# Attention scores of a hybrid decoder: one 32-row matmul per head at four row positions, into four banks, in place of masked copies of the keys

## What is computed

```
att      = einsum('bnthd,bnshd,bntshd->bnhts', q, k, decay)      # causal
o_intra  = einsum('bnhts,bnshv->bnthv', att, v)
o_inter  = einsum('bnthd,bnhdv->bnthv', q * exp(b), S_start)
S        = exp(b_last) * S + sum_s (k * exp(b_last - b)) v
o        = o * rsqrt(mean(o^2) + eps)                            # per head
```

## Time and profile before

| | |
|---|---|
| median of 3 runs | 1743.29 us (1737.36 to 1917.84) |
| the profiled execution | 1752.2 us |
| its span on the slowest core (core 0) | 1750.7 us |
| spans of the other cores | 1719.4 to 1745.9 us |
| PE busy in the span | 1589.6 us (91%) |
| DVE / ACT / POOL busy | 910.9 / 766.9 / 148.1 us |
| mean granted TensorE clock, core 0 | 0.950 |

### The profile page before, as it was taken

How to read it: one execution, slowest core, us unless ns; L and a number is a source line. 1 busy time by engine, 2 the same in 40 slices (tenths; PEclk the granted TensorE clock), 3 DMA queues, 4 the chain that set the end, 5 groups by cost and what they waited for, 6 DMA issues and landing times.

```text
span 1750.7 us, 27970 instructions; the slowest of 8 cores (1719.4 to 1750.7 us)
## 1 busy us (share of the span) xinstructions
PE 1589.6 (91%) x9214; PEld 852.5 (49%) x9214; DVE 910.9 (52%) x2106; ACT 766.9 (44%) x1470; POOL 148.1 (8%) x178
## 2 busy tenths in 40 slices
PE   5688998887998989898999989999999999968995
PEld 3344454444444545445565444545454544535562
DVE  4547244367316756695334853466336655484215
ACT  3243335437334424745336443545255524634343
POOL 1000100000001030010000110000001030010001
PEclk9677899999999999999999999999999999988998
DMA  9997989984898498663797777973455453332332
GB/s 169 157 237 165 170 166 234 212 238 152 189 194 250 146 197 182 168 198 106 152 208 203 232 158 217 241 245 117 166 178 183 155 180 125 103 117 97 122 121 83
DMA packets 133963, 303.40 MB, mean 173 GB/s; under 512 B 48174, under 2 KB 98734, under 8 KB 109870
## 3 DMA queue, kind: packets, MB, share of 16 engines
q1 hardware_dynamic: 81278, 244.93, 44.2%
q0 software_dynamic: 52544, 56.69, 24.8%
HBM read 289.37 MB, written 76.48 MB: 209 GB/s over the span
## 4 chain that ended last, share of the span: by engine, by line
PE 75%; DVE 6%; issue 6%; DMA 6%; ACT 5%; SPq 0%; POOL 0%; DVEq 0%; ACTq 0%; POOLq 0%
PE pst L48 75%; DMA s_fr<-w_ff 4%; DVE scr L48 2%; DVE s_acc L48 1%; ACT s_ymix L48 1%; DMA s_mr<-w_in 1%; ACT s_xbF L48 1%; DMA s_fr<-wc 1%; ACT scr L48 1%; ACT s_sring L48 1%; DVE s_nwt L48 1%; ACT s_hbuf L48 1%; ACT s_junk L48 1%; DVE s_fst L48 1%; DVE s_castb L48 1%
## 5 line engine op out<-in xcount | busy, mean ns | idle before, releaser
L48 PE MATMUL pst<-s_xbF,s_fr 128*128 128x512 bf16 (+3 forms) x2816 | 504.4, 338 | 16.2 <-ACT s_xbF L48 12.0
L48 PE MATMUL pst<-s_fr,s_hbuf 128*128 128x512 bf16 x2112 | 474.3, 381 | 10.5 <-ACT s_hbuf L48 8.2
L48 DVE SCALAR_TENSOR_TENSOR s_acc<-s_acc,pst 128x512 f32<-128x512 f32 x340 | 232.7, 686 | 345.3 <-PE pst L48 342.4
L48 PEld LDWEIGHTS pst<-s_xbF,s_fr 128*128 128x128 bf16 x2816 | 276.5, 100 | 218.8 <-issue 32.6
L48 PEld LDWEIGHTS pst<-s_fr,s_hbuf 128*128 128x128 bf16 x2112 | 204.3, 98 | 252.9 <-issue 25.5
L48 ACT ACTIVATE s_sring<-pst 128x512 f32<-128x512 f32 (+3 forms) x324 | 162.6, 502 | 317.6 <-PE pst L48 304.1
L48 PE MATMUL pst<-s_xbM,s_mr 128*128 128x512 bf16 (+2 forms) x1280 | 246.6, 354 | 16.6 <-ACT scr L48 9.4
L48 ACT ACTIVATE scr<-pst 128x512 f32<-128x512 f32 (+9 forms) x259 | 120.9, 476 | 248.2 <-PE pst L48 219.3
L48 ACT ACTIVATE s_hbuf<-s_sring 128x512 bf16<-128x512 f32 (+3 forms) x311 | 165.1, 531 | 31.8 <-DVE s_sring L48 3.9
L48 DVE SCALAR_TENSOR_TENSOR s_acc<-s_acc,s_fst,s_lng 128x1024 f32<-128x1024 f32 x136 | 173.0, 1281 | 10.4 <-POOL s_fst L48 9.4
L48 PEld LDWEIGHTS pst<-s_xbM,s_mr 128*128 128x128 bf16 (+1 forms) x1280 | 109.4, 99 | 131.2 <-issue 40.6
(11 more groups left out here) (132 smaller groups left out, 1076.1 us busy)
## 6 DMA issues: line engine op xcount, KB each, us to landing
s_fr<-wc SPq DMA_DIRECT2D x118, 1024.0 KB, 5.9
s_mr<-wc SPq DMA_DIRECT2D x27, 1024.0 KB, 9.3
wc<-s_fr SPq DMA_DIRECT2D x26, 1024.0 KB, 11.1
s_fr<-w_ff POOLq DMA_DIRECT2D x22, 1024.0 KB, 16.1
x<-s_acc SPq DMA_DIRECT2D x17, 512.0 KB, 6.0
s_acc<-x SPq DMA_DIRECT2D x17, 512.0 KB, 5.7
s_acc<-xp SPq DMA_DIRECT2D x16, 512.0 KB, 7.7
wc<-w_ff POOLq DMA_DIRECT2D x8, 1024.0 KB, 22.9
```

Of the source, the lines that this page charges most:

```text
L48: return lambda e: getattr(e, name)(*a, **k)
```

## The change

`keTm`, its four scaled copies and its space in the scratch buffer go. `scores` now takes a tuple of chunks. It takes all four M banks, one for each head, and issues for each chunk four matmuls whose stationary and moving operands are the 32 partitions of that head (`c(col, n, parts, first partition)`), so that each lies at another row position of the array. The four prompt chunks are done in one call before the chunk loop: 16 matmuls of 128 columns, then four copies and four mask products, now one for each head instead of one for each chunk. `intra` takes its operand from the head's buffer, and waits for all four of them. The planner is told that these matmuls cost a third of the usual, and `MSTART` goes from −0.1 to −0.15.

```diff
-MSTART = -0.1
+MSTART = -0.15
...
-            keTm = arB.carve(4 * NT, BF16)
-            ta_ = [arB.carve(512, BF16)]
-            attm = [arB.carve(512, BF16) for _ in range(2)]
+            ta_ = [arB.carve(512, BF16) for _ in range(2)]
+            attm = [arB.carve(512, BF16) for _ in range(4)]
...
-            for h in range(4):
-                P.either(I("activation", keTm.c(h * NT, NT), keT.c(0, NT), AF.Copy, scale=hm4.c(h, 1)),
-                         I("tensor_scalar", keTm.c(h * NT, NT), keT.c(0, NT), hm4.c(h, 1), None, ALU.mult),
-                         keT.k() + hm4.k(), keTm.k(h * NT, h * NT + NT), NT, 0.4)
...
-            def scores(c, kind):
-                pa = mbank()
-                P.pe([mm(pa.c(h * 128, 128), keTm.c(h * NT + c * 128, 128), qeT.c(c * 128, 128), 128, True, True) for h in range(4)],
-                     keTm.k() + qeT.k(c * 128, c * 128 + 128), pa.k())
+            def scores(cs, kind):
+                n = 128 * len(cs)
+                pa = [mbank() for _ in range(4)]
+                P.pe([(f, u / 3) for f, u in [mm(pa[h].c((c - cs[0]) * 128, 128), keT.c(c * 128, 128, 32, 32 * h), qeT.c(c * 128, 128, 32, 32 * h), 128, True, True)
+                      for c in cs for h in range(4)]],
+                     keT.k(cs[0] * 128, cs[0] * 128 + n) + qeT.k(cs[0] * 128, cs[0] * 128 + n), [k for p in pa for k in p.k()])
                 mk_ = trilb if kind == "p" else sblkb
-                t_, a_ = ta_[0], attm[c % 2]
-                evac(t_.c(0, 512), pa.c(0, 512), pa.k(), t_.k(), 512)
-                P.dve(I("tensor_tensor", a_.ap(0, [[128, 4], [1, 128]]), t_.ap(0, [[128, 4], [1, 128]]),
-                        mk_.ap(0, [[0, 4], [1, 128]]), ALU.mult), t_.k() + mk_.k(), a_.k(), 512, 0.55)
-                return a_
+                for h in range(4):
+                    t_, a_ = ta_[h % 2], attm[h]
+                    evac(t_.c(0, n), pa[h].c(0, n), pa[h].k(), t_.k(), n)
+                    P.dve(I("tensor_tensor", a_.ap(0, [[128, len(cs)], [1, 128]]), t_.ap(0, [[128, len(cs)], [1, 128]]),
+                            mk_.ap(0, [[0, len(cs)], [1, 128]]), ALU.mult), t_.k() + mk_.k(), a_.k(), n, 0.55)
...
+            ak = [k for a_ in attm for k in a_.k()]
...
+            scores((0, 1, 2, 3), "p")
             for c in range(4):
-                a_ = scores(c, "p")
...
-                     + intra(po, o, c, a_),
-                     qeT.k(c * 128, c * 128 + 128) + Sbdb.k(c * 256, c * 256 + 256) + a_.k() + vtm.k(c * 256, c * 256 + 256), po.k())
+                     + intra(po, o, c, c),
+                     qeT.k(c * 128, c * 128 + 128) + Sbdb.k(c * 256, c * 256 + 256) + ak + vtm.k(c * 256, c * 256 + 256), po.k())
...
-                a_ = scores(c, "s")
+                scores((c,), "s")
```

More of the change, by code:

```diff
@@ L1046, in emit_M @@
                              skip_group_check=True) for q in range(4)], qs.k() + sb.k(), po.k())
-                P.pe(intra(po, 0, c, a_), a_.k() + vtm.k(c * 256, c * 256 + 256), po.k())
+                P.pe(intra(po, 0, c, 0), ak + vtm.k(c * 256, c * 256 + 256), po.k())
                 finish(po, c, 1, 2)
```

4 lines of the change are left out of this document (2 added, 2 removed).

## The result

The changed kernel takes 1754.47 us (median of 4 runs, 1752.15 to 1755.08), the kernel before 1740.62 us beside it on the same chip: ratio 1.0083, 95% interval [1.0061, 1.0106]. It is slower by 14 us, where the forecast was 1732 us, 11 us less than the 1743 us known then. The time lies inside the range; the sign is wrong. The ratio leaves out executions in a second, slower state that the chip falls into whatever the kernel, such as the one of 1917.84 us before.

A forecast was written before the change was run, and what follows sets the result against it. PE's matmul stream, busy 1589.6 of 1750.7 us, was taken as the bound. Terms -4.0 - 1 - 4 - 5 + 6 - 4 - 2 + 1 = -13 us gave 1731 us as a median, forecast as 1732; range 1708 to 1760.

The forecast's parts named there:

- Scores, -4.0 us: Attention scores on PE: four row positions overlap, less 0.26 us extra a burst; -4.0 us, ends -6.6 and +2.6.
- Masked copies, -1 us: Masked key copies on ACT and DVE: already hidden, removal only frees the engines a little; -1 us, ends 0 and -5.7.
- The sign given for them: Sign of being right: the masked copies gone from ACT and DVE, with ACT's busy time some 14 us less.
- M(0,0), -4 us: First attention stage, 50 to 77 us: more projection cover against new mask waits; -4 us, ends -9 and +3.
- DMA queues, 0 us, ends -6 and +8: Transfers: same ones in another order, a store moved ahead can only free a ring slot earlier; 0, ends -6 and +8.
- Head of F(0,1), -4 (ends -9, 0): Stretch 380 to 434 us: 80 projection matmuls instead of 32 ahead of the first transposes shrink idle time; -4 us.
- F(0,2), +6 (ends 0, +12): Stretch 547 to 604 us: projections between its matmuls go, attention matmuls that wait for DVE come; +6 us.
- Attention elsewhere, -5 us: Attention outside M(0,0): F's matmuls now between scores and `intra` in nearly all stages; -5 us, ends -11 and +5.
- F(1,3), -2 us: Last head: 12 small matmuls and eight of the projection now come before PE's 7.27 us wait; -2 us.
- Rival B: Scores don't overlap, as their weight loads go one after another; 1737 or 1746 us, chance 0.25.
- Rival C: Four M banks taken at once stall PE at the state product behind the scores, 20 us; 1771 us, chance 0.13.
- The last sign of being wrong: Waits for `s_fr<-wc` or `s_fr<-w_ff` lasting tens of microseconds, meaning the order of transfers decided, not the scores.

The follow-up runs named there:

- full-row kernel: The changed kernel with each score matmul reading all 128 rows instead of its head's 32; ratio to the kernel before 1.0117.
- pairs in M(0,1): The changed kernel with scores written for two chunks at a time in M(0,1) only, four in the other stages; ratio to the kernel before 0.9970.
- the short loads: 14 of 16 loads of F(0,0)'s feed-forward weights bring 2 of 8 slices: changed kernel 0.9991, kernel before 0.9956, both against the kernel before.

## Why the prediction was wrong

The packed scores and the copies were priced rightly, and what the new lists do to transfers and waits was not. By its steps:

- **Scores, -4.0 us:** right. 4.4 us by the bursts (0.55 each), 6, good to 5, by the full-row kernel. The way there was less right. A burst holds PE for 0.34 us, 0.12 over four rounds of 0.055, and not the 0.26 over them that I took from the gate projection; that figure was a mean of busy times at both levels of the clock. At 271.79 us with pairs in M(0,1) eight gate matmuls hold PE for 0.54 us, 0.11 over two rounds of 0.216. The Trainium skill's rule that a change of tiling mode drains TensorE (TensorEngine Tiling (Array Packing), Key Properties) is thereby bounded here at 0.12 us a burst. By the Trainium skill's figure for a load (TensorE: Matmul & The Clock Gate, LDWEIGHTS) an estimate for sixteen loads one after another is 1.7 us, and for four at a time 0.43; the trace disagrees with both, as all sixteen loads are issued in 0.23 us and the whole burst is over in 0.34.
- **Masked copies, -1 us:** right within the error (0.9986 with them thin). They hid. The sign given for them, 14 us less on ScalarE, didn't come: ScalarE is busy 3.6 us less and VectorE 9.9, since the planner deals their other work anew.
- **M(0,0), -4 us:** PE is through with the stage's work at 89.34 us in the mean of the cores instead of 91.21 (on the two slowest at 89.75 and 95.65), so some 2 us came. The waits didn't shrink: 3.44 and 6.45 us now instead of 6.32 and 2.21; the clock is better (0.75 instead of 0.62). And the gain was lost at once: the next stage's input rows land at 96.9 us instead of 92.4, and PE starts on them at 97.1 instead of 93.2. The step priced the attention and not the transfer behind it.
- **DMA queues, 0 us, ends -6 and +8: the step that failed.** I reasoned that a store of weights ahead of the transposing load could only free a ring slot earlier, and wrote that weights are asked for by PE's place in the list, and took 0. With the store ahead these rows land 4.4 us later (and later too in the two other kernels looked at that have it). And M(0,2)'s weights, asked for by PE's place, land 34.8 and 28.6 us after their issue on the slowest core, where 21.1 and 15.7 had been enough before. Waits for transfers up to F(0,0)'s end grew from 7.8 to 22.3 us in the mean of the cores, +14.5, 8.2 of it for M(0,2)'s weights and 6.2 for the input rows behind M(0,0); on the slowest core M(0,2) alone waits 20.05 us. Over the whole span they grew from 13.8 to 22.6, +8.8, because the wait for `s_fr<-wc` at F(0,1)'s head went from 4.1 to 0.3. I had looked at window 0 of SP's list and not at M(0,2)'s loads, which stand in a stretch where the DMA share was 1.02 already before. The rest of the first column's 19 us isn't taken apart; PE's waits for VectorE up to F(0,0)'s end grew too, from 23.1 to 33.5 us, and those for ScalarE fell from 31.2 to 29.1.
- **Head of F(0,1), -4 (ends -9, 0), and F(0,2), +6 (ends 0, +12):** both signs right, both sizes beyond their ends: -14.5 (3.8 of it the DMA wait) and +13.6. I had seen the 80 projection matmuls ahead of F(0,1)'s transposes and booked them as cover. They are M(0,3)'s, whose gate projection stands at 389.95 us, not M(0,2)'s as I wrote, and so the same matmuls were then missing ahead of F(0,2)'s.
- **Attention elsewhere, -5 us:** wrong. The 256-column group waits 23.8 us instead of 14.7, the transposes 0.9 instead of 6.5, `s_fr,s_xbM` 6.4 instead of 2.4, the scores 2.0 instead of 3.4: 33.1 us instead of 27.0, and without M(0,0)'s two waits 23.2 instead of 18.5.
- **F(1,3), -2 us:** right in size. Its stretch is idle for 18.9 us instead of 20.8, though the first wait only fell from 7.27 to 6.64. The gain of the start, 11 us over F(1,1) to F(1,3), was one of the largest terms of all, and the working hadn't named the rest of it.

Rival B fell with the bursts. Rival C, slower by 20 us because four banks are taken at once, had the sign but not the mechanism. The wait right behind the scores stands in four of the eight stages, 0.85 to 0.96 us each, 3.6 us in all where 20 were priced, and four-chunk calls in seven of eight stages run at 0.9970. What was missing among the rivals is the one that came: the planner reads cheaper scores and fewer operations, deals a whole stage and its loads anew, and the loads meet full queues. The last sign of being wrong was near it, but named loads of `s_fr` and not of `s_mr` and `s_xbM`.

## What stays open

That the form isn't what makes the change slower, and that M(0,2)'s weights land late in five of the slow lists, is shown. Why a load takes 34.8 us to land in one list and 17.7 in another, both at a DMA share near 1, is shown only so far as other loads are part of it (the short loads). By a difference of two timed ratios, good to 7 us, the short loads account for 8 of the 14 us; by the table, for 2 of 19. Whether the store ahead of M(0,1)'s input rows is what delays them wasn't isolated, and pairs in M(0,1) run at 0.9970 with the latest rows of all. What sets F(0,2)'s 17 to 45 us is only partly its cover. And the start of -0.15 is worth 19 to 22 us beside the new scores (two pairs of kernels) and nothing that was timed on the kernel before, whose trace with the early start yet shows 14 us less in F(1,1) and F(1,2), 10 over F(1,1) to F(1,3).

## What to carry to other kernels

Where a planner writes the order, price a change by what the new lists do to every stage and to every load, not by what the new instructions cost: the 4 to 6 us of the edit drowned in terms of 14 to 19 us of both signs, most of them in the heads of F, which have none of the edit's instructions. Where a stage moves into a stretch whose DMA share is 1.0, follow its loads to their landing, not to their issue, before booking the move as cover. Before a row that stands for several instructions is read as a duration, ask for a window with one of them in it. And when a good edit comes out slower, try another form of it that leaves the lists nearer to where they were: two chunks at a time turned +0.8% into -0.7%.
